# The attention branch's output projection moved ahead of the convolution branch's, with gates and normalization placed later

## What is computed

```python
mod = silu(c) @ w_ada + b_ada                    # shift1, scale1, gate1, shift2, scale2, gate2
h   = rms_norm(x, norm1_g) * (1 + scale1) + shift1
u   = h @ w_in                                   # conv (2 x 1024) | q | k | v | gates (2 x 1024)

y   = a * sigmoid(gt)                            # convolution branch
y   = causal depthwise conv, width 31, + conv_b
y   = silu(layer_norm(y))                        # mean and variance over the 1024 channels
y_conv = y @ w_conv_out + b_conv_out

o   = 8 heads of differential attention: (softmax_1 - lam * softmax_2) @ v   # causal, 256 tokens
y_attn = rms_norm(o, subln_g) * (1 - lam_init) @ w_attn_out

g_conv, g_attn = sigmoid(g + b_gate)
x   = x + gate1 * ((g_conv * y_conv + g_attn * y_attn) @ w_o)
h2  = rms_norm(x, norm2_g) * (1 + scale2) + shift2
x   = x + gate2 * moe(h2)                        # top 4 of 32 experts, clamped SwiGLU
```

## Time and profile before

| | us |
|---|---|
| median of three runs | 1286.91 |
| the profiled execution | 1286.41 |
| its span, first to last instruction | 1284.6 |
| TensorE busy | 1080.6 (84%) |
| VectorE busy | 404.4 (31%) |
| ScalarE busy | 219.0 (17%) |
| GpSimd busy | 51.7 (4%) |
| DMA, mean over the span | 370 GB/s, 475.81 MB |

### The profile page before, as it was taken

The page is one execution under the profiler, slowest core; times in us unless marked ns, Lnnn a source line. Parts: engine busy times, 40 slices in busy tenths (PEclk is TensorE's granted clock), DMA queues, the critical chain, the costliest instruction groups (busy, mean ns, idle before and its releaser), DMA issues.

```text
span 1284.6 us, 23431 instructions
## 1 busy us (share of the span) xinstructions
PE 1080.6 (84%) x9958; PEld 528.3 (41%) x9958; DVE 404.4 (31%) x1129; ACT 219.0 (17%) x461; POOL 51.7 (4%) x91
## 2 busy tenths in 40 slices
PE   8999999899998566669998657968669696999975
PEld 5864458788433122224443212423224242444431
DVE  1388997631232111112222111212112121232221
ACT  1111124640121000002211001201002110122110
POOL 2000000355000000000000000000000000000000
PEclk9999999999999887889999888989889898999998
DMA  9998672256879999999999999999999999599997
GB/s 328 349 371 327 239 285 92 106 181 228 325 323 427 428 427 428 427 427 429 426 429 427 427 428 427 426 425 429 428 427 429 425 429 427 241 429 428 428 426 312
DMA packets 66084, 475.81 MB, mean 370 GB/s; under 512 B 6329, under 2 KB 19966, under 8 KB 39390
## 3 DMA queue, kind: packets, MB, share of 16 engines
q1 hardware_dynamic: 62100, 471.36, 89.2%
q0 software_dynamic: 816, 1.84, 0.5%
q10 hardware_dynamic: 3098, 1.56, 0.5%
HBM read 473.03 MB, written 1.05 MB: 369 GB/s over the span
## 4 chain that ended last, share of the span: by engine, by line
PE 49%; DMA 41%; SPq 5%; ACT 3%; DVE 1%; another core or an unknown queue 1%; issue 1%; ACTq 0%; DVEq 0%
DMA weights<-in_w_down 27%; PE bank L1556 14%; DMA weights<-in_w_up 13%; PE bank L1288 7%; PE bank L1584 7%; PE bank L1281 6%; SPq L462 4%; PE bank L1273 2%; PE bank L1426 2%; PE bank L1498 2%; PE bank L1224 2%; PE bank L1485 1%; PE bank L1194 1%; DMA weights<-in_w_ada 1%; PE bank L1505 1%
## 5 line engine op out<-in xcount | busy, mean ns | idle before, releaser
L1556 PE MATMUL bank<-weights,buf_d 128*32 128x512 f32 x3008 | 394.6, 671 | 141.6 <-DMA weights<-in_w_up 141.6
L1556 PEld LDWEIGHTS bank<-weights,buf_d 128*32 128x32 f32 x3008 | 96.9, 117 | 405.0 <-DMA weights<-in_w_up 211.5
L1584 PE MATMUL bank<-weights,buf_d 128*32 128x256 f32 x3008 | 177.6, 382 | 42.7 <-DMA weights<-in_w_down 39.9
L1165 DVE TENSOR_SCALAR u_conv<-bank 128x256 f32<-128x256 f32 x47 | 20.0, 425 | 467.5 <-PE bank L1556 467.5
L774 ACT ACTIVATE u_conv<-u_conv 128x256 f32<-128x256 f32 x47 | 19.6, 416 | 708.5 <-DVE u_conv L1165 708.5
L1584 PEld LDWEIGHTS bank<-weights,buf_d 128*32 128x32 f32 x3008 | 90.7, 110 | 115.5 <-DMA weights<-in_w_down 51.6
L864 DVE SCALAR_TENSOR_TENSOR weights<-u_conv,weights 128x256 f32<-128x256 f32 x240 | 97.8, 481 | 0.5
L1281 PE MATMUL bank<-weights,buf_d 128*128 128x512 f32 x192 | 82.9, 594 | 0.0
L1177 DVE TENSOR_TENSOR buf_d<-bank,u_conv 128x256 f32<-128x256 f32 x47 | 20.0, 425 | 180.1 <-PE bank L1584 180.1
L774 ACT ACT_TABLE_LOAD x47 | 60.3, 1283 | 1.4 <-issue 0.5
L1288 PE MATMUL bank<-buf_d,weights 128*128 128x256 f32 x256 | 58.6, 383 | 0.0
(11 more groups left out here) (274 smaller groups left out, 799.4 us busy)
## 6 DMA issues: line engine op xcount, KB each, us to landing
weights<-in_w_up SPq DMA_DIRECT2D x128, 2048.0 KB, 35.5
weights<-in_w_down SPq DMA_DIRECT2D x64, 2048.0 KB, 39.2
weights<-in_w_in SPq DMA_DIRECT2D x10, 2048.0 KB, 15.5
weights<-in_w_ada SPq DMA_DIRECT2D x8, 2048.0 KB, 19.3
weights<-in_w_ada SPq DMA_DIRECT2D x8, 1024.0 KB, 11.3
weights<-in_w_in SPq DMA_DIRECT2D x8, 512.0 KB, 10.1
weights<-in_w_in SPq DMA_DIRECT2D x4, 1024.0 KB, 13.1
weights<-in_w_conv_out SPq DMA_DIRECT2D x2, 2048.0 KB, 11.3
```

Of the source, the lines that this page charges most:

```text
L1556: ins = t.matmul(UP[SLOTS * g:SLOTS * g + SLOTS, :], xgT[:, r, SLOTS * j:SLOTS * j + SLOTS], up_group(w[:, r, :], g), start=False, stop=(j ...
L1584: ins = t.matmul(DOWN[rows, 0:T], actT[:, r, at:at + SLOTS], w[:, g, r, T * q:T * q + T], start=False, stop=(h == 1 and g == 1 and r == 1))
```

## The change

Four things are changed together. The blocks of w_attn_out are loaded and used ahead of those of w_conv_out, and the order of the PSUM banks, of the slots for the first chunks and of SyncE's waits follows. In the loop over heads TensorE computes gate h - 1 where it computed gate h; gate 7 comes after the last attend. Mean and variance of the convolution come two heads later, its swish sigmoids after the copies of `oT`, between the two halves of the gates' sigmoids, and the convolution's last taps are spread over heads 0 to 3 where they were in 0 and 1. VectorE multiplies the attention's gates first and the convolution's after them, with the add of the two behind the latter.

```diff
@@ -48,7 +48,7 @@
 PARTS = 5
-MEAN_AT, VAR_AT = 2, 4
+MEAN_AT, VAR_AT = 4, 6
 ALPHA = 1.702
@@ -57,7 +57,7 @@
 GATE_SLOT, VALUE_SLOT, HEAD_SLOT, CONV_SLOT, SMALL_SLOT = 6, 7, 8, 9, 10
-SLOT_ORDER = (0, VALUE_SLOT, 1, HEAD_SLOT, 2, 3, CONV_SLOT, GATE_SLOT, 4, 5, SMALL_SLOT)
+SLOT_ORDER = (VALUE_SLOT, 0, 1, 2, 3, CONV_SLOT, GATE_SLOT, HEAD_SLOT, 4, 5, SMALL_SLOT)
 MASKED = -1e30
@@ -292,10 +292,10 @@
         blocks += [block_of(w_in, NB * i) for i in range(10, 14)]
+        AOUT0 = len(blocks)
+        blocks += [block_of(w_attn_out, 0), block_of(w_attn_out, NB)]
         COUT0 = len(blocks)
         blocks += [block_of(w_conv_out, 0), block_of(w_conv_out, NB)]
-        AOUT0 = len(blocks)
-        blocks += [block_of(w_attn_out, 0), block_of(w_attn_out, NB)]
         WO0 = len(blocks)
@@ -343,17 +343,14 @@
         order += [("ada", 1)] + [("v", i) for i in range(4)] + [("mod2T", 0), ("mod2T", 1)] + [("qkT", i) for i in range(8)]
-        for h in range(HEADS + 1):
-            if h < HEADS:
-                order += [("gate", h)]
-            if h:
-                order += [("aT", h - 1), ("o", h - 1)]
+        for h in range(1, HEADS):
+            order += [("gate", h - 1), ("aT", h - 1), ("o", h - 1)]
             if h == MEAN_AT:
...
                 order += [("var", 0)]
-        order += [("y_conv", i) for i in range(3)] + [("oT", i) for i in range(4)] + [("y_conv", 3)]
-        order += [(name, i) for name in ("y_attn", "w_o") for i in range(4)]
+        order += [("aT", HEADS - 1), ("o", HEADS - 1), ("gate", HEADS - 1)]
+        order += [(name, i) for name in ("oT", "y_attn", "y_conv", "w_o") for i in range(4)]
         order += [("x1T", i) for i in range(4)]
@@ -461,20 +458,19 @@
-            sp.wait_ge(*used[COUT0])
+            full(sp, OT_USE + 3)
             load_chunk(0, 0)
-            full(sp, OT_USE + 3)
-            load_chunk(0, 1)
-            sp.wait_ge(*used[COUT0 + 1])
-            load_chunk(0, 2)
-            sp.wait_ge(ebias_ready, 3 * PARTS)
-            load_chunk(0, 3)
             for i in range(2):
                 sp.wait_ge(*used[AOUT0 + i])
-                load_chunk(0, 4 + i)
-            full(sp, YA_USE + 3)
+                load_chunk(0, 1 + i)
+            for i in range(2):
+                sp.wait_ge(*used[COUT0 + i])
+                load_chunk(0, 3 + i)
+            full(sp, YC_USE[3])
+            load_chunk(0, 5)
+            sp.wait_ge(mixed, 4)
             load_chunk(1, 0)
-            sp.wait_ge(mixed, 4)
+            sp.wait_ge(ebias_ready, 3 * PARTS)
             load_chunk(1, 1)
@@ -687,6 +683,12 @@
+            def keep_gate(h):
+                use = gate_use(h)
+                full(act_e, use)
+                s.activation(gates[:, 2 * h, :], bank(use)[:, 0:T], ACT.Identity, bias=cols[:, 40 + 2 * h:41 + 2 * h])
+                s.activation(gates[:, 2 * h + 1, :], bank(use)[:, T:2 * T], ACT.Identity,
+                             bias=cols[:, 41 + 2 * h:42 + 2 * h]).then_inc(bank_free[use % 4], 1)
@@ -699,12 +701,7 @@
                     keep_aT(h - 1)
-                use = gate_use(h)
-                full(act_e, use)
-                s.activation(gates[:, 2 * h, :], bank(use)[:, 0:T], ACT.Identity, bias=cols[:, 40 + 2 * h:41 + 2 * h])
-                s.activation(gates[:, 2 * h + 1, :], bank(use)[:, T:2 * T], ACT.Identity,
-                             bias=cols[:, 41 + 2 * h:42 + 2 * h]).then_inc(bank_free[use % 4], 1)
-                if h:
+                    keep_gate(h - 1)
                     attended(h - 1)
@@ -713,22 +710,27 @@
                         bank_free[VAR_USE % 4], 1)
-                if h == VAR_AT + 1:
-                    act_e.wait_ge(ln_ready, 1)
-                    for k in range(KD):
-                        s.activation(u_conv[:, k, 0:T], conv_acc[:, k, :], ACT.Sigmoid, scale=cols[:, 8 + k:9 + k],
-                                     bias=cols[:, 16 + k:17 + k]).then_inc(sw_sig, 1)
             keep_aT(HEADS - 1)
...
             s.activation(rstd[:], ssq[:], ACT.Sqrt, scale=1.0 / VD, bias=eps[:]).then_inc(o_ready, 1)
-            for i in range(2):
-                s.activation(gates[:, KD * i:KD * i + KD, :], gates[:, KD * i:KD * i + KD, :], ACT.Sigmoid).then_inc(gate_ready, 1)
+            keep_gate(HEADS - 1)
             for i in range(4):
...
+            def sigmoid_gates(first):
+                s.activation(gates[:, first:first + KD, :], gates[:, first:first + KD, :], ACT.Sigmoid).then_inc(gate_ready, 1)
+            act_e.wait_ge(bank_free[gate_use(HEADS - 1) % 4], gate_use(HEADS - 1) // 4 + 1)
+            sigmoid_gates(KD)
+            act_e.wait_ge(ln_ready, 1)
+            for k in range(KD):
+                s.activation(u_conv[:, k, 0:T], conv_acc[:, k, :], ACT.Sigmoid, scale=cols[:, 8 + k:9 + k],
+                             bias=cols[:, 16 + k:17 + k]).then_inc(sw_sig, 1)
+            sigmoid_gates(0)
@@ -942,7 +944,7 @@
             conv(2, 17, TAPS)
-            conv(3, 0, 11)
+            conv(3, 0, 8)
@@ -954,7 +956,7 @@
                 bank_free[M2T_USE[1] % 4], 1)
-            conv(3, 11, 19)
+            conv(3, 8, 14)
@@ -973,8 +975,8 @@
                 v.tensor_scalar(smax[:, par, :], smax[:, par, :], -(HD ** -0.5), None, ALU.mult).then_inc(s_max, 1)
-                if h < 2:
-                    conv(3, (19, 26)[h], (26, TAPS)[h])
+                if h < 4:
+                    conv(3, (14, 18, 23, 28)[h], (18, 23, 28, TAPS)[h])
                 dve.wait_ge(exp_done, 4 * h + 4)
@@ -1023,7 +1025,13 @@
+            for i in range(4):
+                use = YA_USE + i
+                full(dve, use)
+                ga = gates[:, KD + 2 * i:KD + 2 * i + 2, :]
+                v.tensor_tensor(ga, ga, bank(use)[:, :].rearrange("p (c t) -> p c t", t=T), ALU.mult).then_inc(bank_free[use % 4], 1)
+            dve.wait_ge(gate_ready, 2)
             for i in range(4):
@@ -1031,15 +1039,10 @@
                 ins.then_inc(bank_free[YC_USE[i] % 4], 1)
-            dve.wait_ge(gate_ready, 2)
-            for i in range(4):
-                use = YA_USE + i
-                full(dve, use)
-                m = gates[:, 2 * i:2 * i + 2, :]
-                ga = gates[:, KD + 2 * i:KD + 2 * i + 2, :]
-                v.tensor_tensor(ga, ga, bank(use)[:, :].rearrange("p (c t) -> p c t", t=T), ALU.mult).then_inc(bank_free[use % 4], 1)
-                freed(dve, use)
-                v.tensor_tensor(mixT[:, 2 * i:2 * i + 2, :], m, ga, ALU.add).then_inc(mixed, 1)
+                freed(dve, YA_USE + i)
+                freed(dve, YC_USE[i])
+                v.tensor_tensor(mixT[:, 2 * i:2 * i + 2, :], gates[:, 2 * i:2 * i + 2, :], gates[:, KD + 2 * i:KD + 2 * i + 2, :],
+                                ALU.add).then_inc(mixed, 1)
@@ -1351,6 +1354,14 @@
+            def gate_half(h, j):
+                n = GATE0 + h // 2
+                if j == 0:
+                    if h % 2 == 0:
+                        wait_block(n)
+                    fill(pe, gate_use(h))
+                channels(gate_use(h), n, h % 2, j, h1T)
@@ -1364,15 +1375,10 @@
                 ins.then_inc(sc_full, 1)
-                if h % 2 == 0:
-                    wait_block(GATE0 + h // 2)
-                n = GATE0 + h // 2
-                fill(pe, gate_use(h))
-                channels(gate_use(h), n, par, 0, h1T)
                 if h:
+                    gate_half(h - 1, 0)
                     turn(h - 1)
-                channels(gate_use(h), n, par, 1, h1T)
-                if h:
+                    gate_half(h - 1, 1)
                     attend(h - 1)
@@ -1386,6 +1392,8 @@
             attend(HEADS - 1)
+            for j in range(2):
+                gate_half(HEADS - 1, j)
@@ -1394,9 +1402,6 @@
-            pe.wait_ge(swish_ready, KD)
-            for i in range(3):
-                conv_out(i)
             pe.wait_ge(on_ready, 1)
@@ -1405,7 +1410,6 @@
                 ins.then_inc(bank_full[use % 4], 1)
-            conv_out(3)
             for i in range(4):
@@ -1414,6 +1418,9 @@
                     channels(YA_USE + i, AOUT0 + i // 2, i % 2, j, oT)
+            pe.wait_ge(swish_ready, KD)
+            for i in range(4):
+                conv_out(i)
             wait_block(WO0)
...
             for i in range(4):
```

## The result

The changed kernel takes 1291.74 us (median of eight runs, 1290.08 to 1293.67) where the kernel before, run beside it, takes 1287.48 (eight runs, 1286.76 to 1288.06). The ratio is 1.0034, with an interval of 1.0023 to 1.0045: 4.3 us slower, by more than the 2.6 us that count as a difference here. The forecast was 1289.7, slower, in a range of 1286.3 to 1292.0. The profiled execution took 1292.54 us, its span 1290.7.

The account below looks back on a forecast made before the run. The prediction took the expert weight stream, started by the first unit after TensorE's mixer work, to bound the end. Holes of +1.7, +0.6, +1.7 and -1.1 made 2.9 us, 2.8 by the timeline: 1286.91 + 2.8 = 1289.7, range 1286.3 to 1292.0.

Parts of the forecast that it names:

- The bound: Expert weight stream waits for the first unit, so a mixer ending x us later moves the end by x.
- First head: Ahead of head 0's aT transposes: a new TensorE hole waiting for VectorE's softmax, +1.7 us, bounds 0.5 and 3.
- Heads 1 to 7: Head loop: the normalization's two holes move two heads down at the same size; the swish's hole goes, -1.1 us.
- Tail of the heads: Attend(6) to attend(7)'s end, now without a gate between: 3.4 us where it was 2.81, +0.6, bounds 0 and 1.3.
- After the heads: Between the oT transposes and the attention's projection: a hole waiting for ScalarE's copies, +1.7 us, bounds 1.1 and 2.6.
- The sum: All holes together: 2.9 us by the holes, 2.8 by the timeline, giving 1289.7 us.
- Transfers: Loads of weight chunks: chunk 7 waits for the split biases until 340 us, which costs nothing.
- (1): Covers hold better: first head's hole 0.5, that before the projection 1.1; +1.1 us in all, 1288.0 us; chance 0.20.
- (2): Faster: all three holes in the heads go as ScalarE is never behind; -2.3 us, 1284.6 us; chance 0.14.
- (4): Split biases so late that chunks 7 to 9 delay the stream's start; 4 us more, 1293.7 us; chance 0.04.
- rival (3): TensorE's granted clock falls behind one of the new holes; 1.8 us more, 4.6 in all, 1291.5 us; chance 0.10.

Follow-up runs that it names:

- e5_delay: The kernel before with 31 idle matmuls (5.0 us) put ahead of w_o; median 1291.89 us over seven runs, against 1287.74 for the kernel before.
- e8_ln: The kernel before with VectorE's two wide normalization steps put behind the next head's maxima instead of ahead of them; 1284.28 us, ratio 0.9970.
- e1_again: The changed kernel run once more, unaltered, for its spread; 1292.69 us over five runs, ratio 1.0037 to the kernel before.
- e3_taps: The changed kernel with no convolution taps in head 0, those moved to heads 1 to 3; 1290.04 us over nine runs, against the changed kernel's 1291.74.
- e6_order: The changed kernel with normalization, swish and taps put back, leaving only the new order of gates and projections; 1296.27 us, ratio 1.0062 to the kernel before.
- e10_lnwarm: The kernel before with the normalization's wide steps behind the next maxima and five idle matmuls at the routing's end; 1284.4 us, ratio 0.9987.
- e11_all: The changed kernel without head 0 taps, with oT copies on two engines, wide steps behind next maxima, idle matmuls behind head 6 and in routing; 1285.55 us.
- e7_warm: The kernel before with five idle f32 matmuls in TensorE's two longest waits at the end of the routing; 1286.7 us, ratio 0.9998.
- e2_fill: The changed kernel with ten idle matmuls behind head 6, five ahead of head 7's transposes and five ahead of its attend step; 1291.26 us.
- e4_ot: The changed kernel with two of the four oT copies on VectorE in place of ScalarE; 1290.86 us over six runs.
- e12_best: The kernel before with wide steps behind next maxima and the convolution projection's first block split around the last head's transposes; 1285.52 us, ratio 0.9988.
- e9_hot: The changed kernel with idle matmuls behind head 6, behind the oT transposes and at the routing's end; median 1290.09 us over nine runs.

## Why the prediction was right, and where it was off

- **The bound.** Right. The stream of expert weights starts with the first unit, and the end follows: 5.0 us put in gave 4.2 to 5.4 at the end (e5_delay), and w_o 2.85 us earlier gave 2.9 from lower group to lower group and 3.5 by the medians (e8_ln). The profiles say it more sharply. In the six in which neither the first unit nor the last chunk lost anything (before, e1_again, e3_taps, e6_order, e10_lnwarm, e11_all), w_o starts anywhere from 319.27 to 331.73 us, and from there to the end of the span it is always 962.4 to 962.7 us.
- **First head.** Right in kind: 1.74 us of idle time (1.89 by starts) where 1.7 was forecast, VectorE's taps as the cause (e3_taps, and 4.57 us in e6_order, with the old 14 tap instructions, against 4.6 by the same working).
- **Heads 1 to 7.** Right. The holes of the normalization moved two heads down and kept their size (1.42 and 1.04 us), that of the swish went. From attend(0) to attend(6) it took 59.43 us; the prediction's terms add up to 59.4. So the table loads that went with the swish gave back nothing beyond the 1.1 us of that hole.
- **Tail of the heads.** 3.4 us forecast from attend(6) to the end of attend(7), 3.52 where the clock held.
- **After the heads.** A hole of 1.81 us where 1.7 was forecast. Gate 7, transposes and hole together took 10.62 us at the upper level, 10.46 by the forecast's terms.
- **The sum.** 2.8 us forecast, 3.36 measured at the upper level. The first head, the tail and the part after the heads were each 0.1 to 0.2 short, and the eight blocks took 55.33 where 55.25 was forecast, all on the same side.
- **Transfers.** The split biases were ready at 329.30 + 2.44 = 331.7 us, not at 340: the loads that GpSimd waits for landed faster, and it waited 2.3 and 2.4 us for the last two where it was 8.6 and 6.2 before. It cost nothing, as said.
- **Rivals (1), (2) and (4).** The first head's hole and that before the projection were 1.74 and 1.81 us, not 0.5 and 1.1; the normalization's two holes stayed; and the first unit came 5.19 us later (368.61 against 363.42) where w_o came 5.03 later, so no transfer held it up.
- **The missing part is rival (3)**, to which I gave 0.10 and a price of 1.8 us: a fall of the granted clock behind the new holes. In the profiled execution 0.67 us on attend(7) and 0.92 on gate 7 were lost this way, in e1_again's nearly as much (0.67 and 0.85) and 1.7 more behind the oT copies, and in e6_order's 1.6 behind the 4.57 us of the first head. The argument against it, that holes of up to 1.41 us in the heads left the clock at the upper level, was too narrow. Those ended 10 to 11 us apart, while the new ones end at 256.21, 257.81 and 258.99, and then there is one more. That it is this closeness that matters is argued, not shown. The Trainium skill (TensorE: Matmul & The Clock Gate, Part 1) tells of a kernel in which TensorE idled briefly between groups of matmuls often enough for the rate to swing between its two levels. The trace agrees in so far as the granted clock was 0.50 from 258.9 to 262.0 us, behind three short holes. The rival should have been weighed as a chance per execution.
- **Not in the prediction: the first unit.** In the profiled execution of the change 1.07 us are lost behind w_o. The queue of SyncE shows it; the merged row's end is the issue of the chunk that waits for the first 16 matmuls.

```profile
367.79 4.54 SPq L459 DMA_DIRECT2D weights<-in_w_down  x2
```

Two chunks take from 367.79 to 372.33 to be issued; before it was 4.06 us, and 2.95 to 3.1 us where the first unit runs at the upper level (e1_again, e3_taps, e7_warm). At the lower level the slot comes free so late that the stream, by all appearance, has a gap:

```profile
373.79:375.79 2.00, 2.00 (x24) 0.63 (x20) 0.00 (x0) 0.00 (x0) 0.00 (x0) 1.00 0.92 320
```

320 GB/s in these 2 us where 427 is the mean later on the earlier trace rows, and the rest of the stream is late by 1.0. From that first issue to the last expert's it took 866.5 to 867.0 us in nine profiles and 867.6 to 867.9 in the four in which these two issues took 4.3 us or more (after, e2_fill, e4_ot, e8_ln). The lower level alone isn't enough: before and e12_best had it too, with 4.06 and 4.04 us for the two issues, and lost nothing. e8_ln is the kernel before with two steps moved, so the loss isn't the change's alone. It may be the cause of the middle group of before; no profile of before in that group was taken, so this is argued, not shown.

So the 4.3 us are 3.4 us of holes and, by what is left, 0.9 us of clock, unevenly spread over the executions. The forecast's side held, and its value was low by the clock and by 0.6 us of small terms. That the range held is in part luck: the same kernel's second set of runs has its median at 1292.69, above the upper end of 1292.0, and so has all thirteen runs together (1292.35).

## What to carry to other kernels

Where a long stage bound by transfers follows a short one, lay out the busiest engine's instructions of the short stage in order, look up at each wait what it waits for, and add the holes. Of twelve times foretold here ten were met to within 1.3 us. The changed kernel itself came 2.0 above its forecast, by the clock, by small terms and by 0.6 us of the kernel before, and e12_best 2.5, where the rival, a wait for a bank, came true. A time that is met isn't yet a mechanism that is: in e4_ot and e11_all the lengths of the mixer spoke for the rival, though the medians lay near the theory. A wide step of another branch belongs behind the small step for which a third engine waits: two moves of such steps on VectorE won 2.8 us. And short holes can cost more than their length, since the clock may fall behind them.

## What the runs showed of the hardware that I had not expected

- The same program loses the clock at a given place in some executions and not in others. Gate 7 took 6.9 us in two of four profiled executions with the same holes ahead of it (e3_taps, e4_ot), and 7.8 in the other two. Medians of five to nine runs of such a kernel scatter by 1 us (1291.74 and 1292.69 for the same program).
- The last matmuls of the kernel, those on the last chunk, took 1.98 us where TensorE had waited 1.15 us for it (before) and 3.68 where it had waited 4.21 (e9_hot), and the combine behind them 1.24 or 2.18. The chunk's landing itself differs by up to 1.5 us between executions.
- A hole of 4.57 us was followed by some 3 us at 1.2 GHz, 1.6 us lost (e6_order), as much as the three short ones ahead of gate 7 cost in the profiled execution of the change.
- Where the first unit ran at the lower level, the rest of the stream was late by 1.0 us in four profiles and by nothing in two. In these six, 4.04 and 4.06 us for the two issues cost nothing, and 4.29 us and more did.
